# Attention scores with masks last, paired retention heads and one activation table set in a two-block transformer kernel

## What is computed

```python
# stick-breaking heads, per block of 128 queries
z = einsum('bhqd,bhkd->bhqk', qb, k) * scale
mask = kpos[None, :] < qpos[:, None]
lneg = where(mask, log_sigmoid(-z), 0.0)
tail = cumsum(lneg, axis=3, reverse=True) - lneg
w = where(mask, exp(log_sigmoid(z) + tail), 0.0)
out = einsum('bhqk,bhkd->bhqd', w, v)
# retention heads, chunks of 128
scores = einsum('bhnid,bhnjd->bhnij', qc, kc) * dmat
inner = einsum('bhnij,bhnjd->bhnid', scores, vc)   # + the state of the chunks before
y_b = group_norm(y_b) * silu(r_g)
x = x + concatenate([y_a, y_b], -1) @ w_out
```

## Time and profile before

| | us |
|---|---|
| three runs | 1622.66, 1623.78, 1623.96 |
| median | 1623.78 |
| span of the profiled execution, first to last instruction | 1621.5 |
| PE busy | 1487.6 (92%) |
| DVE, ACT, POOL busy | 468.2, 421.6, 459.8 |
| core's mean granted TensorE clock | 0.981 |

### The profile page before, as it was taken

How to read it: one execution, slowest core, us unless ns; L and a number is a source line. 1 busy time by engine, 2 the same in 40 slices (tenths; PEclk the granted TensorE clock), 3 DMA queues, 4 the chain that set the end, 5 groups by cost and what they waited for, 6 DMA issues and landing times.

```text
span 1621.5 us, 18760 instructions
## 1 busy us (share of the span) xinstructions
PE 1487.6 (92%) x7596; PEld 850.5 (52%) x7597; DVE 468.2 (29%) x807; ACT 421.6 (26%) x530; POOL 459.8 (28%) x356
## 2 busy tenths in 40 slices
PE   8998899998898988899888999887999998999998
PEld 7777533333333333333233333333798776789986
DVE  6427511211111111111111111112357187233311
ACT  6364310101001001010010010013555643453332
POOL 6815000000000000000000000003588563779994
PEclk9999999999899999999999999999999999999999
DMA  9521699999999999999999999999455331545540
GB/s 349 196 90 52 267 430 428 428 428 427 426 428 428 428 428 427 426 428 428 428 428 427 427 427 428 428 427 357 137 183 179 107 100 69 174 152 189 189 167 26
DMA packets 91174, 502.31 MB, mean 310 GB/s; under 512 B 7835, under 2 KB 38163, under 8 KB 66387
## 3 DMA queue, kind: packets, MB, share of 16 engines
q1 hardware_dynamic: 89600, 498.71, 76.1%
q10 hardware_dynamic: 1491, 2.36, 0.5%
HBM read 500.00 MB, written 1.05 MB: 309 GB/s over the span
## 4 chain that ended last, share of the span: by engine, by line
PE 58%; DMA 30%; DVE 5%; ACT 3%; issue 2%; POOL 1%; SPq 1%; DVEq 0%; ACTq 0%
DMA ring<-in_w_up_gate 28%; PE PS L863 16%; PE PS L525 9%; PE PS L526 9%; PE PS L527 9%; PE PS L881 6%; PE PS L832 1%; POOL w_low L2200 1%; DMA ring<-in_w_ple_gate 1%; PE PS L1116 1%; SPq L427 1%; PE PS L870 1%; DVE arena L1882 1%; DVE arena L1879 1%; DVE arena L1877 1%
## 5 line engine op out<-in xcount | busy, mean ns | idle before, releaser
L2200 POOL TENSOR_TENSOR w_low<-ring,w_high 128x512 fp32r<-128x512 f32 (+1 forms) x352 | 459.6, 1344 | 1140.5 <-ACT w_high L1243 1140.0
L863 PE MATMUL PS<-ring,arena 128*64 128x512 f32 x2048 | 460.1, 601 | 31.6 <-DMA ring<-in_w_up_gate 31.6
L863 PEld LDWEIGHTS PS<-ring,arena 128*64 128x64 f32 x2048 | 142.7, 138 | 332.8 <-issue 271.7
L881 PE MATMUL PS<-ring,arena 128*64 128x512 f32 x1024 | 235.3, 613 | 28.0 <-ACT arena L1381 28.0
L1372 ACT ACTIVATE arena<-arena 128x512 f32<-128x512 f32 x32 | 20.1, 629 | 766.1 <-DVE arena L1876 766.1
L1243 ACT ACTIVATE w_high<-ring 128x2048 fp32r<-128x2048 f32 (+1 forms) x89 | 166.4, 1881 | 117.3 <-PE PS L527 101.9
L881 PEld LDWEIGHTS PS<-ring,arena 128*64 128x64 f32 x1024 | 75.2, 140 | 166.0 <-issue 166.0
L1876 DVE TENSOR_SCALAR arena<-PS 128x512 f32<-128x512 f32 x32 | 22.1, 691 | 467.3 <-PE PS L863 467.3
L525 PE MATMUL PS<-w_high,XNT_h 128*128 128x512 f32 (+1 forms) x336 | 136.1, 405 | 8.6 <-DVE XNT_l L1599 7.8
L525 PE MATMUL PS<-XNT_h,w_high 128*128 128x256 f32 (+1 forms) x464 | 131.3, 283 | 3.5 <-DVE XNT_l L1589 2.6
L526 PE MATMUL PS<-w_low,XNT_h 128*128 128x512 f32 (+1 forms) x336 | 132.6, 395 | 0.0
(11 more groups left out here) (364 smaller groups left out, 1458.4 us busy)
## 6 DMA issues: line engine op xcount, KB each, us to landing
ring<-in_w_up_gate SPq DMA_DIRECT2D x128, 2048.0 KB, 23.6
ring<-in_w_down SPq DMA_DIRECT2D x64, 2048.0 KB, 22.2
ring<-in_w_in SPq DMA_DIRECT2D x35, 1024.0 KB, 5.4
ring<-in_w_gate_up SPq DMA_DIRECT2D x22, 1024.0 KB, 5.2
ring<-in_w_down SPq DMA_DIRECT2D x11, 1024.0 KB, 4.9
ring<-in_w_out SPq DMA_DIRECT2D x8, 1024.0 KB, 5.1
ring<-in_w_ple_gate SPq DMA_DIRECT2D x4, 1024.0 KB, 22.1
ring<-in_w_ssd_proj SPq DMA_DIRECT2D x4, 1024.0 KB, 5.0
```

Source lines behind the costliest of these rows:

```text
L863: ins = nc.tensor.matmul(PS[64 * (n % 2):64 * (n % 2) + 64, 4 + n // 2, :], x, w[:, n * 512:(n + 1) * 512], start=False, stop=c == KC - 1, ...
L881: ins = nc.tensor.matmul(PS[64 * n:64 * n + 64, 7, :], lhs, w[:, k, n * 512:(n + 1) * 512], start=(j, k) == (0, 0), stop=(j, k) == (1, 3))
L2200: ins = nc.gpsimd.tensor_tensor(LOW[raw_slot(key)][:, at], slot(raw_slot(key))[:, at], HIGH[m % BUF][:, at].bitcast(F32), ALU.subtract)
```

## The change

Four edits:
- `sb_z` makes the key products of both heads first (256 columns for both, then 128 columns for both), and the four mask products last. The second key product of a head now says start=False: it falls on columns of the bank that the first product's start has cleared.
- `ret_scores(h)` makes the scores of heads h and h + 1, and is called for 0, 2, 4 and 6; the pair 4/5 comes behind the value products of head 1, the pair 6/7 behind those of head 3. The wait is on `ret_w` of h - 2.
- ScalarE loads the set `natural_log_exp_and_others`, named by hand, before the first softplus.
- It does so again in the second block, before the Abs, Exp, Ln and Exp of the time steps (L1449 to L1452).

```diff
@@ sb_z
+                q, k = ([t3(x, 4)[64 * hh:64 * hh + 64, b, :] for hh in range(2)] for x in QKT[:2])
                 for hh in range(2):
-                    q = t3(QKT[0], 4)[64 * hh:64 * hh + 64, b, :]
-                    k = t3(QKT[1], 4)[64 * hh:64 * hh + 64, b, :]
-                    nc.tensor.matmul(PS[:, 4 + hh, 0:256], k[:, 0:P], q, start=True, stop=False)
-                    nc.tensor.matmul(PS[:, 4 + hh, 0:P], ident, cc(C_NEG), start=False, stop=True)
-                    nc.tensor.matmul(PS[:, 4 + hh, 256:384], k[:, P:256], q[:, P:256], start=True, stop=False)
-                    ins = nc.tensor.matmul(PS[:, 4 + hh, 256:384], ident, cc(C_NEG), start=False, stop=True)
+                    nc.tensor.matmul(PS[:, 4 + hh, 0:256], k[hh][:, 0:P], q[hh], start=True, stop=True)
+                for hh in range(2):
+                    nc.tensor.matmul(PS[:, 4 + hh, 256:384], k[hh][:, P:256], q[hh][:, P:256], start=False, stop=True, skip_group_check=True)
+                for hh in range(2):
+                    nc.tensor.matmul(PS[:, 4 + hh, 0:P], ident, cc(C_NEG), start=False, stop=True, skip_group_check=True)
+                    ins = nc.tensor.matmul(PS[:, 4 + hh, 256:384], ident, cc(C_NEG), start=False, stop=True, skip_group_check=True)
                 ins.then_inc(sem("sb_z"), 1)
@@ ret_scores
-                    pe.wait_ge(sem("ret_w"), h - 3)
+                    pe.wait_ge(sem("ret_w"), h - 2)
...
-                q = t3(QKT[2], 4)[64 * (h % 2):64 * (h % 2) + 64, h // 2, :]
-                k = t3(QKT[3], 4)[64 * (h % 2):64 * (h % 2) + 64, h // 2, :]
-                nc.tensor.matmul(PS[:, 2 + h % 4, 0:256], k[:, 0:P], q, start=True, stop=True)
-                nc.tensor.matmul(PS[:, 2 + h % 4, 256:384], k[:, P:256], q[:, P:256], start=True, stop=True).then_inc(sem("ret_s"), 1)
-
-            ret_scores(0), ret_scores(1)
+                q, k = ([t3(x, 4)[64 * odd:64 * odd + 64, h // 2, :] for odd in range(2)] for x in QKT[2:])
+                for odd in range(2):
+                    nc.tensor.matmul(PS[:, 2 + h % 4 + odd, 0:256], k[odd][:, 0:P], q[odd], start=True, stop=True)
+                for odd in range(2):
+                    nc.tensor.matmul(PS[:, 2 + h % 4 + odd, 256:384], k[odd][:, P:256], q[odd][:, P:256], start=True,
+                                     stop=True).then_inc(sem("ret_s"), 1)
+
+            ret_scores(0)
             sb_pv(3)
-            ret_scores(2), ret_scores(3)
+            ret_scores(2)
...
-                if h + 4 < NH:
-                    ret_scores(h + 4)
+                if h in (1, 3):
+                    ret_scores(h + 3)
@@ scalar
             group_out(4)
+            nc.scalar.preload_act_table_set("natural_log_exp_and_others")
             sb_softplus(0)
...
                 if c == 0:
 
+                    nc.scalar.preload_act_table_set("natural_log_exp_and_others")
                     act.wait_ge(sem("dt_abs"), 1)
                     link(nc.scalar.activation(DTA, DT, ACT.Abs))
```

## The result

The changed kernel takes 1614.58 us, the median of 4 runs from 1612.96 to 1615.37, against 1623.87 for the kernel before on the same chip (4 runs, 1622.66 to 1624.07): a ratio of 0.994, with an interval of 0.9929 to 0.9952, so 9.3 us less. The forecast was 1613.0. The profiled execution took 1613.87 with a span of 1611.8, against 1621.5 before: 9.7 us less.

The account below looks back on a forecast made before the run. The expert stage runs at its loads' speed, so TensorE's gains before the first refill count: 7.4 + 1.9 + 1.5 = 10.8 us off the 1621.5 span gives 1610.7, plus 2.3 to the median: 1613.0, range 1609.5 to 1617.0.

Parts of the forecast that it names:

- Step 1: Stick-breaking scores, four blocks: with masks last a block's scores take 1.75 us, not 3.59, saving 7.36 us in all.
- Step 2: Table set named before block 0's softplus: TensorE's waits at the tail sums of blocks 0 and 2 go, 1.91 us.
- drain of 1.38: Alternative price of the added table load before block 0's softplus: 1.38 us more, for a total gain of 10.4.
- The rival that the loads stay: ScalarE's softplus: the named set is exchanged at the first Exp or Ln; gain 8.1 us, time 1615.7, chance 0.07.
- Step 3: Retention heads 4 to 7 scored in pairs: DVE reaches the first gain product 1.5 us earlier; bounds 0.3 and 1.9.
- The margins of the prediction: Slack before conversion becomes late: 0.6 us at piece 13, 0.2 at block 2's tail, 0.4 at the Silu.
- Step 4: Second named load, at the time steps: worth nothing under GpSimd's and TensorE's work, 2.6 us at most without that cover.
- One sign of being wrong: Ahead of the expert stage: the first refill moving by less than the first gain product (L1738) would count against the forecast.
- the rival of the clock: TensorE before the expert stage: the 1.2 GHz level comes earlier and lasts, making the kernel slower; 1634.6, chance 0.02.
- the one stretch more or less that every case had been allowed: One low-clock stretch of TensorE ahead of the expert stage, 1.6 us, taken into the range of every case.
- Conversion: Weight-piece splits on ScalarE and GpSimd become the bound before the expert stage; price 1 to 2 us, 1614.5, chance 0.13.
- The expert stage took nothing back: Opposing rival: loads in the expert stage have room to catch up, so the gain is lost; 1623.8, chance 0.03.

Follow-up runs that it names:

- the three steps alone: Three kernels, each the kernel before with one part only: scores with masks last (1616.00 us), first named table set (1622.08 us), retention scores in pairs (1622.31 us).
- step 1 alone: The kernel before with the masks made last in the stick-breaking scores and nothing else: 1616.00 us, ratio 0.9954.
- step 3 alone: The kernel before with the retention scores in pairs and nothing else: 1622.31 us, ratio 0.9989.
- The filled kernel: The changed kernel plus unread products in TensorE's three gaps (before group norm's result, behind transposes, before router's masks): 1611.87 us, and 1612.05 us when run again.
- the third chip: The changed kernel run again unaltered, beside its versions with filled gaps: 1613.14 us (7 runs), ratio 0.9923.
- the second experiment: The kernel before with only the first named table set, ahead of the first softplus: 1622.08 us (10 runs), ratio 0.9993; its profiled execution took 1624.9.

## Why the prediction was right

Each mark of the prediction, and what the trace of after shows:

| mark | before | predicted | after |
|---|---|---|---|
| a block's scores, us | 3.59 | 1.75 | 1.77 |
| tail sum, block 0 | 87.88 | 85.2 | 85.37, no gap |
| tail sum, block 2 | 113.21 | 105.8 | 105.96, no gap |
| first gain product | 138.46 | 127.7 | 127.89 |
| output projection, second half | 157.17 | 146.4 | 146.83 |
| first refill | 195.13 | 184.3 | 185.43 |
| span | 1621.5 | 1610.7 | 1611.8 |

**Step 1** held in mechanism and size: 3.59 to 1.77, and alone it moved the retention scores by 7.2 and the median by 7.8. The pair of retention heads in the earlier trace rows had been the right row to read the price from.

**Step 2** held: the gaps of 0.71 and 0.88 are gone, they return without the named set, and they were worth 0.87 and 1.12 (0.87 and 1.04 in the sum). Taking 0.16 more than the bracket shows was right. (By its own numbers the prediction's sum for a drain of 1.38 is 84.3 + 1.4 = 85.7, not 85.6; nothing hangs on it.) The load cost 1.28 with 0.02 behind it, also where it directly follows a copy. The rival that the loads stay is out: 520 ScalarE instructions, 10 fewer than before.

**Step 3** held for DVE: 1.44 against 1.5. The margins of the prediction were met as well: 0.55 at piece 13 (0.6), 0.48 between Silu's end and the gain product (0.4).

**Step 4** showed no gain. In after the four operations from 1182.18 us on stand behind one load. No run changes this load alone, but from the refill to the end, where it lies, the four traces without it (before and the three steps alone) have 1425.8 to 1426.6 us, and the ten with it 1425.7 to 1427.4.

**One sign of being wrong came true**: "a refill that moves by less than L1738 did". L1738's successor moved by 10.57 and the refill by 9.70. The sum had the whole gain pass from the gain product to the refill, and 0.87 of it did not: the gain product became slower and the clock was low for longer. The expert stage took nothing (901.91 against 902.28 us). So the cause of the gain was right, and the error lies in those two terms, which the sum had at nothing.

**Where 1.1 us went** between the sum (10.8) and the trace (9.7), by the marks of this one execution:
- 0.18 before the change begins: the scores of block 0 start at 77.93, not at 77.75. With it the gain product is 10.57 earlier; from the start of the scores it is 10.75, so the three steps together missed their sum by 0.06.
- 0.23 on the gain product itself. It takes 1.51 us and took 1.28. GpSimd is at work beside it in both kernels (in after from 123.35, for 11.93 us), but it meets GpSimd's quarters at another point. The sum had kept its duration. The steps alone tell where this comes from: with single retention heads (step 1 alone) it takes 1.28, with the pairs (step 3 alone) 1.51. The rows give the rest: GpSimd's next quarter starts 0.15 us after the gain product in the first case and 0.36 to 0.40 in the second, and the 0.23 are that difference.
- 0.64 in the clock. From the second half's start to the refill it was 37.96 us and is 38.60. The prediction had seen that TensorE's gap before the transposes grows by 0.4: it is 2.05 us in after, and was 1.63. The first product behind the gaps took 0.50 and takes 0.80 now, and from 146 to 151 the granted clock is 0.50 flat. In after the first 11 starts fill 4.83 us where they would fill 0.34 + 10 x 0.233 = 2.67 at the full clock: 2.16 lost. In before the clock fell only at the third product: 10 starts in 3.96 for 2.44, 1.52 lost. The difference is 0.64. This is the rival of the clock in small, with the one stretch more or less that every case had been allowed. It was put into the range and not into the sum. The size is that of one pair of executions: the second trace of after has 39.14 us in this stretch, not 38.60. The direction is firmer. The two traces with single retention heads and no fall in the heads have a gap of 1.63 and 1.64 before the transposes and then 37.96 and 37.42 us; the eight with pairs and nothing in the gap have 2.04 or 2.05 and then 38.38 to 39.45.

The filled kernel shows the size of that last term from the other side: with the clock at 1.00 the refill comes 2.75 earlier, and would come earlier still if GpSimd did not then hold up the second half.

**The other rivals.** Conversion did not become the bound of after; one new wait for GpSimd, 0.51 for the weight load at 135.33, lies under the chain through DVE, which releases TensorE at 143.25. It does become the bound once the clock is mended (1.07 at 153.44). The expert stage took nothing back: 901.91 against 902.28 us. The median differed from the forecast by 1.6 us in the result (1614.58): 1.1 in the span, and 0.5 because the median lies 2.8 above the span of the profiled execution, where 2.3 had been taken. That it differed by only 0.1 on the third chip (1613.14) is luck in part: the profiled execution there has a span of 1612.4, 1.7 above the forecast one, and was the slowest of its seven runs.

**What stays open** is what decides in which execution the clock falls. In the second experiment it fell for 13.7 us with PE busy; in after it didn't at the same heads; in one trace of the filled kernel it fell once and in another it did not. The spread of the medians, some 1.5 us, fits this. The mean clock of each run points the same way in the four runs of the result (0.983, 0.981, 0.980 and 0.979 from the fastest to the slowest) but not in every set (with the three gaps filled again, 0.985 at 1610.32 and at 1612.84 us); and only the profiled executions show their clock in time, so it is argued and not shown.

## What to carry to other kernels

Put products that use half of the array's rows together and those that use all of it behind them: here a block's scores fell from 3.59 to 1.77 us, 1.17 of it from six changes of shape less and 0.65 from heads side by side. A stage that is saturated by DMA hands on what is gained in front of it in full, if its first transfer waits for the engine that gained, so look for that issue and price everything by when it comes. Where a change makes the work in front of a wait shorter, read the granted clock behind the wait too: here 0.4 us more of idleness went with 0.4 to 2.0 us more in the stretch behind it, and a few products that nobody reads gave back 2.75 at the refill in one trace and some 1.8 in the median.

## What was not expected of the hardware

- **Half-row products overlap without standing side by side in the program.** With head 0's two products in front of both of head 1's, the scores take 1.78 us, and alternating 1.77. The Trainium skill (TensorE: Matmul & The Clock Gate, "Part 3: Packing small matmuls — row/col tiling") says that products keep the order of the program in both start and end. By that, head 1's first product could not begin before head 0's second, 0.54 us after head 0's first by the earlier trace rows (132.53 - 131.99), and the scores would take some 0.5 more, an estimate from those rows. The trace does not agree: nothing is added, and head 1's first product is recorded 13 ns behind head 0's, before head 0's second; that the compiler put them in another order is not excluded, but the 13 ns, 6 or 7 in after, speak against it.
- **A change of shape costs 0.20 us**, by the earlier trace rows, and the kernel with the heads in turn agrees with it: 0.195. The Trainium skill (TensorEngine Tiling (Array Packing), "Key Properties") names a drain at a change of mode and no price; that such a drain is what the 0.20 us are, no run shows.
- **A table load has no drain beside it here.** It ends at 79.59 + 1.28 = 80.87 and Abs starts at 80.89. The page that asks for 1.38 more (the Trainium skill, ScalarE: Activation LUTs, "What ACT_TABLE_LOAD costs") would have Abs start at 82.25.
- **TensorE's clock can fall while the records show it busy**: 0.50 from 132.2 to 145.9 us in the second experiment, with PE busy 13.70 us of 13.70. What the engine did before and in it are products of 64 columns and the short scores of the heads; the gap of 1.13 us that ends at 127.26 stands in before too (at 129.28), and there the clock stayed at 1.00. In after the same work stayed at 1.00.
- **DVE's product of 128x1024 in f32 has no one duration beside GpSimd**: the two gain products took 1.28 and 2.17 in before, 1.51 and 2.19 in after, and in the second experiment 1.96 and then, with GpSimd done, 1.22. The recorded starts of GpSimd's quarters of a piece tell on what it hangs. In all thirteen traces in which both gain products meet GpSimd, the product takes what is left until GpSimd's next quarter starts, plus 1.12 to 1.15 us: 0.15 left gives 1.28, 0.37 gives 1.51, and 1.06 to 1.08 gives 2.17 to 2.20. And GpSimd's quarter that starts beside such a product takes 2.26 to 2.29 in place of 1.28. So each seems to wait for the other's running instruction; no run moves one of them by itself.
